# One opening stage for three, and attention value products one item later, in a four-layer float32 model on one core

## What is computed

```
cos, sin = rope_tables(positions)              # angle = position * inv_freq
c_act = silu(c)
for l in range(2):                             # first block
    mod = c_act @ w_ada[l] + b_ada[l]          # 6 x 1024 values
    sh_m, sc_m, g_m, sh_f, sc_f, g_f = split(mod, 6)
    h = x * (1 + sc_m) + sh_m
    mix = token_mixers(h, w_in[l], ...)        # h @ w_in; sparse attention of 8 heads, retention, mLSTM
    ...                                        # output product, norm, 16 experts, norm
# second block: layer 0 without attention; layer 1:
#   chunk_band_attention of 16 heads: softmax(q k' + bias) v
```

## Time and profile before

| what | value |
|---|---|
| median of 3 runs | 3954.59 us (3952.55 to 3960.49) |
| the profiled execution: its own time | 3954.67 us |
| its span on the core | 3952.9 us |
| TensorE matmul busy | 3380.4 us (86%) |
| VectorE busy | 2309.6 us (58%) |
| ScalarE busy | 1319.4 us (33%) |
| GpSimd busy | 603.6 us (15%) |
| DMA | 401.34 MB, mean 102 GB/s |

### The profile page before, as it was taken

How to read it: one execution, slowest core, us unless ns; L and a number is a source line. 1 busy time by engine, 2 the same in 40 slices (tenths; PEclk the granted TensorE clock), 3 DMA queues, 4 the chain that set the end, 5 groups by cost and what they waited for, 6 DMA issues and landing times. The chain is left out here.

```text
span 3952.9 us, 43316 instructions
## 1 busy us (share of the span) xinstructions
PE 3380.4 (86%) x16912; PEld 2721.9 (69%) x16912; DVE 2309.6 (58%) x3607; ACT 1319.4 (33%) x1864; POOL 603.6 (15%) x538
## 2 busy tenths in 40 slices
PE   4987778998987778998973987879999997799998
PEld 3873557886872557886843875667778787677787
DVE  6868655995668655995447664454443433543534
ACT  2122524773122523773111112113222314632222
POOL 0015500000015500001003341201100102511000
PEclk8986787999996787999986987789999998889999
DMA  5630003992530003991210000002222221122222
GB/s 211 260 118 0 1 17 129 374 375 80 204 116 0 1 16 122 375 375 67 96 70 0 1 1 1 1 1 96 81 96 96 85 86 49 28 87 79 96 96 75
DMA packets 59532, 401.34 MB, mean 102 GB/s; under 512 B 6721, under 2 KB 8385, under 8 KB 12225
## 3 DMA queue, kind: packets, MB, share of 16 engines
q1 hardware_dynamic: 53568, 356.62, 24.6%
q0 software_dynamic: 5760, 41.95, 2.9%
HBM read 396.45 MB, written 2.10 MB: 101 GB/s over the span
## 5 line engine op out<-in xcount | busy, mean ns | idle before, releaser
L135 PE MATMUL ps<-t_part,weight_hi 128*128 128x512 f32 x2160 | 864.3, 400 | 73.8 <-DVE scr_part L171 46.6
L137 PE MATMUL ps<-t_part,ring_lo 128*128 128x512 f32 x2160 | 852.1, 394 | 0.0
L136 PE MATMUL ps<-scr_part,weight_hi 128*128 128x512 f32 x1648 | 651.0, 395 | 0.0
L338 DVE TENSOR_TENSOR ring_lo<-ring,weight_hi 128x2048 fp32r<-128x2048 f32 x133 | 305.5, 2297 | 387.3 <-ACT weight_hi L331 387.3
L135 PEld LDWEIGHTS ps<-t_part,weight_hi 128*128 128x128 f32 x2160 | 413.7, 192 | 166.7 <-DVE ring_lo L164 77.6
L331 ACT CAST weight_hi<-ring 128x2048 fp32r<-128x2048 f32 x133 | 253.8, 1908 | 694.2 <-PE ps L137 694.2
L137 PEld LDWEIGHTS ps<-t_part,ring_lo 128*128 128x128 f32 x2160 | 412.1, 191 | 88.0
L136 PEld LDWEIGHTS ps<-scr_part,weight_hi 128*128 128x128 f32 x1648 | 316.7, 192 | 69.2 <-issue 3.9
L136 PE MATMUL ps<-big_part,weight_hi 128*128 128x512 f32 x512 | 200.7, 392 | 0.0
L192 POOL TENSOR_TENSOR big<-big 128x512 f32<-128x512 f32 x28 | 48.0, 1712 | 891.5 <-ACT big L185 888.0
L440 DVE SCALAR_TENSOR_TENSOR scr_q<-t,c_act,scr_q 128x256 f32<-128x256 f32 x280 | 135.8, 485 | 10.0
(11 more groups left out here) (603 smaller groups left out, 7229.1 us busy)
## 6 DMA issues: line engine op xcount, KB each, us to landing
ring<-in_w_moe SPq DMA_DIRECT2D x84, 1024.0 KB, 5.0
t<-in_w_moe SPq DMA_DIRECT2D x84, 1024.0 KB, 5.0
ring<-in_w SPq DMA_DIRECT2D x64, 1024.0 KB, 4.8
t<-in_w_ada POOLq DMA_DIRECT2D x40, 1024.0 KB, 5.2
ring<-in_w_in SPq DMA_DIRECT2D x32, 1024.0 KB, 4.9
ring<-in_even_in SPq DMA_DIRECT2D x15, 1024.0 KB, 4.8
ring<-in_qkv SPq DMA_DIRECT2D x12, 1024.0 KB, 4.8
ring<-in_w_ada SPq DMA_DIRECT2D x8, 1024.0 KB, 4.9
```

Of the source, the lines that this page charges most:

```text
L135: pe.matmul(bank, w_hi, x_hi, start=first, stop=False)
L136: pe.matmul(bank, w_hi, x_lo, start=False, stop=False)
L137: return pe.matmul(bank, w_lo, x_hi, start=False, stop=last)
L338: v.tensor_tensor(K.ring_lo[:, g % NSLOT, :], K.ring[:, g % NSLOT, :], K.w_hi[:, n % 2, :].bitcast(F32), ALU.subtract).then_inc(w_lo.up(), 1)
```

## The change

Four things are changed.

1. **One opening stage** takes the place of constants, c_act and ada_first; `modulate` goes too. x comes in four loads, w_ada's first eight blocks go to places of their own, not through the ring, and nothing waits for all loads together. VectorE weighs blocks 0, 2, 4, 6 and 7; TensorE weighs 1, 3 and 5, as products of the block with c_act. The loads of swap, bd, tri and the router become preloads of w_in's stage.
2. **In w_in of layer 0** the input is x, and the scale and shift are applied while it is split (`affine`): ScalarE casts x * scale + shift, VectorE makes h and subtracts. The angles are made beside steps 2 to 5 on VectorE (`Angles`), sine and cosine after step 6 on ScalarE. The positions go to `K.work`.
3. **In `softmax_attention`** a head's value products, their copy and the sum come later in the order, and the splitting of the values moves behind the work of the first four items.
4. **Signals** are shared under fewer names in several stages.

```
+    first = {}
+    if l == 0:
+        K.preloads += [(K.swap[:, :], a["k_swap"]), (K.bd[:, :], a["k_bd"]), (K.tri[:, :, :], a["k_tri"]),
+                       (K.wr[:, :, :], a["w_router"]),
+                       (K.br[:, :], bass.AP(tensor=a["b_router"].tensor, offset=0, ap=[[0, P], [1, 16]]))]
+        first = {"affine": (mod[:, 8:16], mod[:, 0:8], K.h), "beside": Angles(K, a)}
```

The split of w_in's input, on VectorE and ScalarE:

```
+        elif affine:
+            s.activation(x_parts(k)[0], x(k), ACT.Identity, scale=affine[0][:, k:k + 1],
+                         bias=affine[1][:, k:k + 1]).then_inc(x_hi.up(), 1)
...
+        if affine:
+            h, st = affine[2](k), K.sig("v_step")
+            v.tensor_scalar(h, x(k), affine[0][:, k:k + 1], affine[1][:, k:k + 1], ALU.mult, ALU.add).then_inc(st.up(), 1)
+            v.wait_ge(st.sem, st.n)
         v.wait_ge(x_hi.sem, x_hi.at(k + 1))
+        if affine:
+            v.tensor_tensor(x_parts(k)[1], h, x_parts(k)[0].bitcast(F32), ALU.subtract).then_inc(x_lo.up(), 1)
```

The new opening, its core:

```
+    by_vector, by_tensor = (0, 2, 4, 6, 7), (1, 3, 5)
     def sync_(sp):
+        sp.dma_start(K.vecs[:, :], a["vecs"]).then_inc(ld.up(16), 16)
+        for b in range(2):
+            sp.dma_start(places[b], a["w_ada"][0, b, 0]).then_inc(ld_w[b].up(16), 16)
+        sp.dma_start(K.ident[:, :], a["k_ident"]).then_inc(ld_x.up(16), 16)
+        for t in range(ST):
+            sp.dma_start(staging[:, t, :], a["x"][t * P:(t + 1) * P, :]).then_inc(ld_x.up(16), 16)
+        for b in range(2, 8):
+            sp.dma_start(places[b], a["w_ada"][0, b, 0]).then_inc(ld_w[b].up(16), 16)
+    def pe_(pe):
+        def weigh(i, b):
+            pe.wait_ge(ld_w[b].sem, ld_w[b].at(16))
+            for half in range(2):
+                for k in range(8):
+                    ins = pe.matmul(K.ps[:, 6, 2 * i + half:2 * i + half + 1], block(b)[:, k, half * P:(half + 1) * P],
+                                    K.c_act[:, k:k + 1], start=(k == 0), stop=(k == 7))
+            ins.then_inc(tensor_done.up(), 1)
...
+        weigh(0, by_tensor[0])
+        total(0, by_vector[0])
+        pe.wait_ge(ld_x.sem, ld_x.at(16 * (1 + ST)))
+        for c in range(4):
+            turn(c)
+        total(1, by_vector[1])
+        weigh(1, by_tensor[1])
+        for c in range(4, 8):
+            turn(c)
+        total(2, by_vector[2])
+        weigh(2, by_tensor[2])
+        total(3, by_vector[3])
+        total(4, by_vector[4])
     def v_(v):
...
+        v.wait_ge(sigmoid.sem, sigmoid.at(1))
+        v.tensor_tensor(K.c_act[:, :], K.c_act[:, :], K.vec("c"), ALU.mult).then_inc(act.up(), 1)
...
+        for i, b in enumerate(by_vector):
+            v.wait_ge(ld_w[b].sem, ld_w[b].at(16))
+            ada_part(K, v, block(b), i, done)
...
+        for bank, blocks in ((6, by_tensor), (7, by_vector)):
+            for i, b in enumerate(blocks):
+                v.tensor_tensor(m[:, 2 * b:2 * b + 2], K.ps[:, bank, 2 * i:2 * i + 2], bias[:, 2 * b:2 * b + 2],
+                                ALU.add).then_inc(st.up(), 1)
```

The angles beside w_in (`do` waits for each operation; SP issues positions and invf at the stage's start):

```
+    def v(self, v, n):
+        if n == 2:
+            v.wait_ge(self.loaded.sem, self.loaded.at(32))
+            do(v.tensor_copy(pos, K.pos_i[:, :]))
+            do(v.tensor_scalar(ang, pos, K.invf[:, 0:1], None, ALU.mult))
+            do(v.tensor_scalar(turns, ang, 1.0 / (2 * math.pi), None, ALU.mult))
+        if n == 3:
+            do(v.tensor_scalar(turns, turns, big, None, ALU.add))
+            do(v.tensor_scalar(turns, turns, -big, None, ALU.add))
+        if n == 4:
+            for c in (c1, c2, c3):
+                do(v.scalar_tensor_tensor(out=ang, in0=turns, scalar=-c, in1=ang, op0=ALU.mult, op1=ALU.add))
+        if n == 5:
+            do(v.tensor_scalar(ang, ang, math.pi, -math.pi, ALU.min, ALU.max))
+            do(v.scalar_tensor_tensor(out=absolute, in0=ang, scalar=-1.0, in1=ang, op0=ALU.mult, op1=ALU.max))
+            v.tensor_scalar(absolute, absolute, -1.0, math.pi / 2, ALU.mult, ALU.add).then_inc(self.ready.up(), 1)
```

```
-        for n in range(N + 4):
+        for n in range(N + 5):
...
-            if n >= 7 and n % ST == 3:
-                head(n // ST - 1)
+            if n >= 8 and n % ST == 0:
+                head(n // ST - 2)
...
         for n in range(N):
-            if n < ST:
-                values_lo(n)
             g.wait_ge(rs.sem, rs.at(n + 1))
...
+            if n < ST:
+                values_lo(n)
...
-            if n >= 8 and n % ST == 0 and n // ST - 2 < heads:
+            if n >= 10 and n % ST == 2:
                 head_sum(n // ST - 2)
...
-        for t in range(ST):
-            s.copy(v_parts(None, t)[0], v_raw(t)).then_inc(vh.up(), 1)
...
+            if n < ST:
+                s.copy(v_parts(None, n)[0], v_raw(n)).then_inc(vh.up(), 1)
-            if n >= 8 and n % ST == 0 and n // ST - 2 < heads:
+            if n >= 9 and n % ST == 1:
                 move(n // ST - 2)
```

Shared names, one example, and the embedding's wait:

```
-    qh, kh, vh, ze = K.sig("queries_hi"), K.sig("keys_hi"), K.sig("values_hi"), K.sig("keys_cleared")
+    oh, vh = K.sig("operands_hi"), K.sig("values_hi")
...
-            v.reciprocal(self.inverse, self.inverse).then_inc(self.ready.up(), 1)
+            v.reciprocal(self.inverse, self.inverse).then_inc(K.sig("v_step").up(), 1)
+            v.wait_ge(K.sig("v_step").sem, K.sig("v_step").n)
```

203 lines of the change are left out of this document (88 added, 115 removed).

## The result

The changed kernel takes 3934.3 us (median of 5 runs, 3931.95 to 3939.88) against 3955.4 before (5 runs, 3952.55 to 3960.49): ratio 0.9947, 95% interval 0.9935 to 0.9959. It is faster by 21 us, where 41 were forecast; the time lies 1.3 us above the range. The profiled execution took 3933.85, its span is 3932.1.

The account below looks back on a forecast made before the run. It took TensorE's stands as the bound: serial opening, w_in's ring through three engines, attention waits between VectorE, ScalarE and TensorE. Opening -23.6 and attentions -17.4 from 3954.7 gave 3913.7 us, range 3892 to 3933.

Parts of the forecast that it names:

- D: Rival: clock stays at 1.2 GHz in opening and attentions, making the kernel slower, 3966 us; chance 0.03.
- C: Rival: TensorE slow in the opening, w_in starting at 46 instead of 37.5, kernel 3922 us; chance 0.08.
- w_in at 37.5, -28.0: Opening: w_in's stage starts at 37.5 us instead of 65.53, with TensorE's weighing at the fast clock; -28.0 us.
- +0.55 for the first block: w_in's first block: the modulation moved there makes the first product 0.55 us later.
- The angles, +3.9: w_in's steps 2 to 5: angle operations on VectorE, 6.2 us in all, cost 3.9 by a recurrence of step and weighing ends.
- The opening in all, -23.6: Sum of the opening's terms, including the first block's and the angles' costs in w_in: -23.6 us.
- The attentions, -17.4: Three attentions: 16 periods without key part at -1.25 each and 13 with one at +0.2, TensorE fast; -17.4 us.
- Key periods at 7.85: Attention loop: a head's period where POOL makes key and query parts takes 7.85 us at the fast clock.
- Query periods at 6.55: Attention loop: a head's period where POOL makes only a query part takes 6.55 us, against 7.8 in the present order.
- 13 x +0.2 for the key periods: Attentions: 13 of 29 periods, those with a key part, get 0.2 us longer each, +2.6 us.
- The start, net 0: Attentions' start: first scores 1.1 us earlier, but head 2's operands at the same moment or 0.4 later; net 0.
- Rival A: The attentions give nothing, key parts and exposed products eating the rest; kernel 3931 us, chance 0.20.

Follow-up runs that it names:

- opening_only: The changed kernel with the attentions put back as before (order of products, copy and sum, and the values' split): 3938.9 us, ratio 0.9959 to the kernel before.
- key_early: The changed kernel with only POOL's key low part moved behind item 0, the query part left behind item 1: 3904.4 us, ratio 0.9879 to the kernel before.
- filled_10: The changed kernel with ten unneeded identity turnings on TensorE before it waits for the parts of a head with a key part: 3926.5 us, ratio 0.9924.
- values_back: The changed kernel with the values' split put back ahead of the attention loop (ScalarE's casts, POOL's parts ahead of normalising): 3933.2 us, ratio 0.9954.

## Why the prediction was wrong

The sign and the two mechanisms were right; the size was off by 20 us: 6 to 8.5 in the opening's part and 11.5 to 13 in the attentions'. Most of it is one cause, which I had only as a rival for the attentions (D, 0.03) and for the opening (C, 0.08), and not for w_in: TensorE's clock. Two further terms were mis-sized and work against each other, the key periods and the start.

- **w_in at 37.5, -28.0.** -26.0. Loads, VectorE's blocks and the sums came as worked out, to half a microsecond. The term that failed is TensorE's "4.0 or 8.1 us a block", taken at the fast clock: two blocks of three took 7.0. C's mechanism, a fourth of its size.
- **+0.55 for the first block.** +0.6.
- **The angles, +3.9.** 6.0 by the kernel without them. The recurrence for the stands was right, 1.44 + 2.18 = 3.6 in place of 3.9 us. What it lacked is that TensorE multiplies at the lower level for some 3.5 us behind each: 3.2 to 3.4 us more. And I had asked only what the angles cost there, not whether a line higher they would have had a gap.
- **The opening in all, -23.6.** -17.9 by the trace at the end of w_in, -15.1 (interval some 5 each way) by opening_only.
- **The attentions, -17.4.** -4.6 and -5.9. Key periods at 7.85: 7.82 at the full clock. Query periods at 6.55: 6.56 at the full clock in key_early and filled_10. The walk through four programs was right; the failed step is "TensorE fast", which made "16 x -1.25". The seven query periods of the band attention took 7.5 to 8.3, where most took 7.7 before (3363.47 to 3371.14): they gained nothing, where 8.75 us were forecast for them. I had written down what it costs at the slow clock, 9.6, and that the gap ahead of each key-part head speaks for it, and gave it 0.03 because "TensorE's waits get fewer". Fewer they got, but longer: 14 stands of up to 3.3 us in place of many of 0.2 to 1.7.
- **13 x +0.2 for the key periods.** Six of them in the band attention became 0.7 shorter each, 8.86 to 8.13. The 8.15 that the prediction had for the order of before stands in no row. The head that it had read took 8.87, and the other five took 8.81 to 8.92, all at a lowered clock. So the walk at the full clock was held against a value that none of these periods reached. The six gained 4.4 us where a loss of 1.2 was forecast, and that they cover some of what the query periods missed is luck.
- **The start, net 0.** +1.9 for each attention, 5.7 in all if the second attention is like the two in the table: I had moved the products one item back in the loop and forgotten that the first ones move too. Part of it comes back at the other end, where the heads' stretch is an item shorter; the whole band attention, first scores to last products, gained 1.1. The values' split is net 0, as values_back shows.
- **Rival A** (the attentions give nothing, 3931, 0.20) is nearest to where it ended, by another way than A's: not because key parts and exposed products ate the gain at the full clock.
- **Signs named beforehand.** VectorE's idle before the sums near 0: 6.4. Long periods with TensorE waiting for POOL: yes. POOL's parts took nothing from VectorE that can be seen: the 32 sums took 670 to 695 ns each. Wrong "if the mean period stays at 8": it is 7.7, worked out as the 8.05 was.

## What to carry to other kernels

Where a change makes one long stand of the engine out of several short ones, price the burst behind it at the lower clock too; the granted clock of each stretch of the loop as it is says where the low level lies already, and a walk at the full clock is to be compared with those rows, not with their mean. A wait that is taken out of a loop with two waits gives what the other leaves: look for what is late next on every queue (here POOL's two operations, which had an idle place one item earlier), and mend both before judging either. Side work on an engine in a ring belongs into the place where that engine waits in each round, which can be a line away.

## What the runs showed of the hardware

- Ten turnings of an identity ahead of a wait made the kernel 8 us faster: with their 1.25 us in a stand of 3.3, the granted clock was 1.00 in four of seven periods where it had been 0.69 to 0.86. Without them the same loop (values_back) had one of seven.
- Stands of mostly 2.0 to 2.2 us in every period, with 4.5 us of work between, went with a clock of 1.00 in ten of the first thirteen periods of key_early; stands of 1.91 and 2.65 in the dense w_in were each followed by some 3.5 us at the lower level. So the length of a stand alone doesn't tell it. In the changed kernel the fall came 1.6 us into the burst behind the stand, not at its start.
- In the opening the granted clock in the records was 1.00 in the first block (8.50 to 16.00), while its products ran at the pace of half clock, 6.96 against 3.63 to 3.75 elsewhere. There the durations are the better witness.
- Of identical code, w_in's start varied from 37.0 to 42.7 us and the first attention's heads from 50.4 to 53.3, each with another draw of the clock: the opening's three blocks took 15.7 us together in the first and 20.9 in the second. Differences below 5 us between two traces mean nothing without the clock beside them.
